# Second projection by token: 16 wide products, a copy and 8 transposes in place of 64 products

## What is computed

```python
p = h @ w_in                                  # 1024 -> 2176 columns
u_pool, c_val, c_gate, s_h, s_b, s_c = split(p)
y_a = pool_mixer(u_pool);  z = c_val * sigmoid(c_gate)
y_b = silu(layer_norm(depthwise31(z) + b_dw)) # 31 taps
y_c = s_b * depthwise3(s_c * s_h)             # 3 taps
x = x + concat[y_a, y_b, y_c] @ w_out
h = rms_norm(x);  ids, gates = top 16 of 8 heads' product keys of (h @ w_q)
x = x + sum_k gates_k * gelu(h . expert_u[ids_k]) * expert_v[ids_k]
```

## Time and profile before

| | |
|---|---|
| Median of 3 runs | 3525.51 us (3525.33 to 3532.18) |
| The profiled execution | 3508.12 us, span 3505.7 us |
| Mean granted PE clock | 0.825 of 2.4 GHz |
| PE busy | 2387.2 us (68%), 7990 matmul instructions |
| DVE busy | 2172.2 us (62%) |
| POOL busy | 2141.8 us (61%), 2176 gathers |
| ACT busy | 259.9 us (7%) |
| DMA | 1201.44 MB, mean 343 GB/s; the gather queue holds 86% of the 16 engines' span |

### The profile page before, as it was taken

How to read it: one execution, slowest core, us unless ns; L and a number is a source line. 1 busy time by engine, 2 the same in 40 slices (tenths; PEclk the granted TensorE clock), 3 DMA queues, 4 the chain that set the end, 5 groups by cost and what they waited for, 6 DMA issues and landing times.

```text
span 3505.7 us, 25147 instructions
## 1 busy us (share of the span) xinstructions
PE 2387.2 (68%) x7990; PEld 890.5 (25%) x7990; DVE 2172.2 (62%) x5644; ACT 259.9 (7%) x506; POOL 2141.8 (61%) x2184
## 2 busy tenths in 40 slices
PE   7123876577875875587978366748798764865498
PEld 6112323121311241123314121412332322111022
DVE  3988278866666775735467777772716787655500
ACT  3000100100000000000100100001010000000000
POOL 0365566656665655666566656565656675666665
PEclk9666898788987967798989688669899886878799
DMA  6587898999899989997897999799789899999998
GB/s 236 222 326 297 297 366 313 366 349 378 320 379 360 350 318 409 410 410 290 309 366 292 372 341 387 291 379 355 288 316 362 339 349 348 369 387 385 370 380 330
DMA packets 331598, 1201.44 MB, mean 343 GB/s; under 512 B 40898, under 2 KB 41290, under 8 KB 329418
## 3 DMA queue, kind: packets, MB, share of 16 engines
q0 software_dynamic: 313344, 1140.99, 86.0%
q1 hardware_dynamic: 17034, 49.94, 3.7%
q10 hardware_dynamic: 1088, 8.91, 0.6%
HBM read 1188.82 MB, written 10.87 MB: 342 GB/s over the span
## 4 chain that ended last, share of the span: by engine, by line
PE 23%; another core or an unknown queue 21%; POOL 18%; DVE 17%; issue 14%; DMA 5%; ACT 2%; ACTq 0%; DVEq 0%; POOLq 0%
POOL rows L590 18%; PE acc L974 11%; DVE rows L1420 8%; PE psA L807 4%; DMA rows<-in_expert_v,idsT 4%; PE psB L917 3%; PE psA L798 2%; DVE work L1149 1%; DMA rows<-in_expert_u,ids 1%; DVE work L1235 1%; DVE work L1228 1%; PE psB L834 1%; DMA w_in_sb<-in_w_in 1%; DVE work L1225 1%
## 5 line engine op out<-in xcount | busy, mean ns | idle before, releaser
L974 PE MATMUL acc<-rows,strip 128*32 128x512 f32 x4352 | 1558.1, 654 | 546.8 <-DMA rows<-in_expert_v,idsT 403.3
L1420 DVE CUSTOM_DVE_ANT_0 rows<-rows,psH 128x1024 f32<-128x1024 f32 x1088 | 1290.9, 1218 | 399.7 <-DMA rows<-in_expert_u,ids 296.3
L590 POOL DMA_INDIRECT rows<-in_expert_v,idsT x1088 | 1100.5, 1011 | 667.3 <-issue 268.3
L590 POOL DMA_INDIRECT rows<-in_expert_u,ids x1088 | 1040.3, 956 | 681.6 <-issue 317.3
L974 PEld LDWEIGHTS acc<-rows,strip 128*32 128x32 f32 x4352 | 349.1, 115 | 1633.3 <-issue 1038.4
L807 PE MATMUL psA<-hT,w_in_sb 128*128 128x128 f32 (+1 forms) x1280 | 203.1, 315 | 97.9 <-issue 97.1
L807 PEld LDWEIGHTS psA<-hT,w_in_sb 128*128 128x128 f32 x1280 | 190.6, 231 | 124.0 <-issue 124.0
L1149 DVE SCALAR_TENSOR_TENSOR work<-zbuf,chan,work 128x128 f32<-128x128 f32 (+1 forms) x870 | 215.2, 325 | 6.7 <-DVE work L1149 3.9
L798 PE MATMUL psA<-w_out_sb,hT 128*128 128x512 f32 x320 | 163.0, 651 | 32.7 <-ACTq L661 25.9
L1427 DVE TENSOR_TENSOR x_out<-acc,x_out 128x1024 f32<-128x1024 f32 (+1 forms) x10 | 12.2, 1221 | 266.0 <-PE acc L974 178.6
L917 PE MATMUL psB<-w_q_sb,hT 128*128 128x512 f32 x288 | 141.2, 640 | 31.7 <-remote 15.7
(11 more groups left out here) (181 smaller groups left out, 1287.5 us busy)
## 6 DMA issues: line engine op xcount, KB each, us to landing
rows<-in_expert_u,ids POOLq DMA_INDIRECT x1088
rows<-in_expert_v,idsT POOLq DMA_INDIRECT x1088
w_in_sb<-in_w_in ACTq DMA_DIRECT2D x4, 2176.0 KB, 17.6
w_in_sb<-in_w_in SPq DMA_DIRECT2D x4, 2176.0 KB, 18.6
w_out_sb<-in_w_out SPq DMA_DIRECT2D x2, 4096.0 KB
w_q_sb<-in_w_q SPq DMA_DIRECT2D x2, 4096.0 KB
x_out<-x_mid SPq DMA_DIRECT2D x10, 512.0 KB
x_mid<-x_mix SPq DMA_DIRECT2D x8, 512.0 KB
```

Of the source, the lines that this page charges most:

```text
L590: nc.gpsimd.indirect_dma_start(out=rows[:, j, :], out_offset=None, in_=table[:, :], in_offset=bass.IndirectOffsetOnAxis(ap=index, axis=0))\
L974: last = nc.tensor.matmul(acc[LS * a:LS * (a + 1), half:half + 512], strip[:, first:first + LS], rows[:, at % RING, half:half + 512], star ...
L1420: nc.vector.tensor_tensor_reduce(rows[:, j, :], rows[:, j, :], psH[:, :], 1.0, 0.0, ALU.mult, ALU.add, dots[:, r:r + 1]).then_inc(s_free[j ...
```

## The change

For tiles 1 to 9 the second projection is made by token, as the first one is: for each chunk k, two products of 128x512 with `hT` chunk k as weights (16 products in all), into `psA`. The yields stay. ACT then copies the 128x1024 result into `hT` (tick 9, `KEEP_B`, after `s_pC`, when PE reads `hT` no more), PE turns it back with 8 transposes into `psA` (tick 10, `TURN_B`, before `POOL_MIX`, with a `yield` between them), and the copy of `s_h` moves to tick 11 and waits for the transposes. Tile 0 stays as it was.

```diff
-CONV, PROJ_C, POOLING, SH_COPY, POOL_MIX, POOL_KEEP, SHORT, ... = 8, 8, 9, 9, 10, 11, 12, ...
+CONV, PROJ_C, KEEP_B, POOLING, TURN_B, POOL_MIX, SH_COPY, POOL_KEEP, SHORT, ... = 8, 8, 9, 9, 10, 10, 11, 11, 12, ...
```

```diff
-                if tick == SH_COPY:
+                if tick == KEEP_B and m:
                     act.wait_ge(s_pC, m + 1)
+                    nc.scalar.copy(hT[:, :, :], tri(psA[:, :])).then_inc(s_pBc, 1)
+                if tick == (SH_COPY if m else KEEP_B):
+                    if m:
+                        act.wait_ge(s_pB, m)
+                    else:
+                        act.wait_ge(s_pC, 1)
                     nc.scalar.copy(shc[:, :, 0:L], p_sh[:, :, 0:L]).then_inc(s_sh, 1)
```

```diff
-                if tick in (PROJ_B, PROJ_B + 1):
+                if m == 0 and tick in (PROJ_B, PROJ_B + 1):
                     for k in range(4 * (tick - PROJ_B), 4 * (tick - PROJ_B) + 4):
                         last = project(m, psA, D, k)
+                if m and tick in (PROJ_B, PROJ_B + 1):
+                    for k in range(4 * (tick - PROJ_B), 4 * (tick - PROJ_B) + 4):
+                        for half in (0, 512):
+                            nc.tensor.matmul(psA[:, half:half + 512], hT[:, k, :], w_in[:, k, D + half:D + half + 512],
+                                             start=k == 0, stop=k == DC8 - 1, skip_group_check=True)
                         if k < DC8 - 1:
                             yield
-                    if tick == PROJ_B + 1:
-                        last.then_inc(s_pB, 1)
...
+                if tick == TURN_B and m:
+                    pe.wait_ge(s_pBc, m)
+                    for c in range(DC8):
+                        last = turn(psA[:, c * P:(c + 1) * P], hT[:, c, :])
+                    last.then_inc(s_pB, 1)
+                    yield
                 if tick == POOL_MIX:
```

More of the change, by code:

```diff
@@ L23 @@
 NORM, NORM_ROWS, TURN_X, HT_SET, PROJ_A, PROJ_B, GATE_SIGMOID, HISTORY, GLU = 0, 1, 2, 3, 4, 6, 6, 6, 7
-CONV, PROJ_C, POOLING, SH_COPY, POOL_MIX, POOL_KEEP, SHORT, MEAN, CENTRE = 8, 8, 9, 9, 10, 11, 12, 12, 13
+CONV, PROJ_C, KEEP_B, POOLING, TURN_B, POOL_MIX, SH_COPY, POOL_KEEP, SHORT, MEAN, CENTRE = 8, 8, 9, 9, 10, 10, 11, 11, 12, 12, 13
 OUT_A, OUT_B, SQUARE, VAR, SCALE, SILU, REPEAT, OUT_C, STATES, X1 = 13, 14, 14, 15, 16, 17, 18, 18, 19, 19
@@ L346, in build @@
         s_pA = sem("first_projection_made")
-        s_pB = sem("second_projection_made")
+        s_pBc = sem("second_projection_by_token_copied")
+        s_pB = sem("second_projection_turned")
         s_pC = sem("third_projection_made")
```

## The result

The changed kernel takes 3487.12 us in the median of six runs (3480.56 to 3496.37). The kernel before took 3531.15 us in the six runs beside it (3525.33 to 3548.66). The ratio is 0.9879, with a 95% interval from 0.9857 to 0.9901: faster by about 43 us, between 35 and 50. The forecast was 3487.5.

A forecast was written before the change was run, and what follows sets the result against it. Gathers run at the DMA limit except where POOL waits, 244.8 us of it for slots PE held. Gains of 50 us less 12 added give 38, so 3525.5 - 38 = 3487.5 us, range 3452 to 3528.

The forecast's parts named there:

- The stall goes with the narrow form: Second projection, L807: 97.1 us of PE idle without shown cause goes with wide products, as only the narrow form stalled.
- B: Rival: the stall isn't of the narrow form, prompt tiles keep it, only sample tiles gain; 4 us, 3521; chance 0.12.
- Tiles 4 and 7 run 21 us shorter on PE and give 12 us each: Sample tiles' second projection: PE stretch from 39.0 to 18 us, POOL's two waits nearly go, DVE limits; 24 us together.
- Tiles 6 and 9 give 15 us: Prompt tiles 6 and 9: POOL's waits of 10.42 and 9.40 us go but for a remainder; gains 8 and 7.
- Tile 1 gives 8 us: Tile 1: POOL's 14.74 us wait goes, but DVE's taps then hold a gather, so only 8 us is gained.
- The added part costs 12 us: Copy and 8 transposes: 2.0 us of PE in each of six prompt tiles, 12 us; bounds 0 and 28.
- The sum: All tiles: 24 + 15 + 8 + 2 + 1 = 50 us gained, less 12 added, net 38 us.
- half of B: Share of rival B counted as 0.03 within the 0.76 chance of a time faster by more than 0.2%.
- SHORT in tiles 5 and 8 comes 10 us later, covered by MEAN: DVE's SHORT waits 10 us more, costed at nothing since its next step awaits MEAN; 2 x 10 us if uncovered.
- Rival C: Stalls stay and DVE reaches SHORT before TURN_B is through, `u` rows behind it: slower, 3556 us; chance 0.11.
- POOL's waits on PE fall from 245 to about 190: Sign to look for: POOL's waits for L974, slots that PE held, fall from 245 to about 190 us.
- No change of the time can come from the arithmetic of the prompt tiles: Prompt tiles, full clock: 128 narrow instructions 14.4 us, 32 wide 14.2, so they gain only if the stall goes.

The follow-up runs named there:

- second trace of the changed kernel: The changed kernel run again without an edit, against the kernel before: 3479.83 us against 3522.63, ratio 0.9874.
- second trace of before: The kernel before run again without an edit, against itself: 3519.95 us against 3529.66, ratio 0.9981.
- sample tiles alone: Only tiles 4 and 7 get the new path, the other tiles as in the kernel before: 3501.93 us, ratio 0.9918.
- added part alone: Kernel before with narrow products kept, plus copy, 8 transposes and later copy of `s_h`: 3524.54 us, ratio 1.0003; on the faster chips 3204.86 us, ratio 0.9995.

## Why the prediction was right, and where it was right by luck

The time, 3487.5, and the sign held on chips of the sort on which before was profiled. The mechanism held in part: PE's stretches became shorter as forecast and POOL's waits behind them went, but in the two tiles that gave most, 13 of PE's 20 us were pace, not idle time, and POOL's waits on PE elsewhere remain. Step by step:

**The stall goes with the narrow form.** Right. L858 has 0.0 us of idle time, four 128x128 in place of each 128x512 bring the stall back (122.5 us), and 128x256 brings 21.6 us. B's doubt was half justified all the same: something of the chip is needed too, since the same narrow form does not stall on the second sort. The prediction took the stall as a property of the form, and it is one of form and chip together. It also read the waits too narrowly. "Only the narrow one stalled" leaves out PE's `v` rows, 512 columns wide, with 116.1 us in 85 waits, and L917, which "had none", has 4.4 us in 2. The form makes the stall where the projection stands; it doesn't follow that a wide instruction can't wait in this way.

**Tiles 4 and 7 run 21 us shorter on PE and give 12 us each.** Right, and a little low. The stretch of tile 4 is 18.5 us where 18 was forecast. The granted clock over it went from 0.54 to 0.97. The stall alone had not kept it low: on the second sort PE was busy for 25.20 of the 25.30 us of the narrow products of tile 4, without a stall, and the clock over them was 0.71, in tile 7 even 0.58. POOL's waits on PE there, 10.83 and 11.85 us, are reduced to a single one of 2.31 up to 1340 us, in the timeline of POOL of the changed kernel:

```profile
1325.80 0.93 POOL L591 DMA_INDIRECT rows<-in_expert_u,ids  x1 [2.31 <-PE acc L990]
```

The start of the first projection in tiles 4, 5, 6, 7, 8 and 9 gives the length of one tile. First PE's timeline of before, then that of after:

```profile
1235.39 2.09 PE L834 MATMUL psB<-w_in_sb,hT 128*128 128x512 f32 x4
...
1556.80 1.98 PE L834 MATMUL psB<-w_in_sb,hT 128*128 128x512 f32 x4
...
1826.28 1.98 PE L834 MATMUL psB<-w_in_sb,hT 128*128 128x512 f32 x4
...
2160.12 2.23 PE L834 MATMUL psB<-w_in_sb,hT 128*128 128x512 f32 x4
...
2459.64 1.98 PE L834 MATMUL psB<-w_in_sb,hT 128*128 128x512 f32 x4 [1.79 <-issue]
...
2733.08 2.47 PE L834 MATMUL psB<-w_in_sb,hT 128*128 128x512 f32 x4
```

```profile
1237.69 1.98 PE L841 MATMUL psB<-w_in_sb,hT 128*128 128x512 f32 x4 [0.99 <-DVE hT L1147]
...
1546.52 2.25 PE L841 MATMUL psB<-w_in_sb,hT 128*128 128x512 f32 x4
...
1819.98 2.06 PE L841 MATMUL psB<-w_in_sb,hT 128*128 128x512 f32 x4
...
2149.20 2.98 PE L841 MATMUL psB<-w_in_sb,hT 128*128 128x512 f32 x4
...
2437.56 3.42 PE L841 MATMUL psB<-w_in_sb,hT 128*128 128x512 f32 x4 [3.32 <-DVE hT L1147]
...
2711.34 1.98 PE L841 MATMUL psB<-w_in_sb,hT 128*128 128x512 f32 x4
```

Tile 4 went from 321.4 to 308.8 us, tile 7 from 299.5 to 288.4: 13 and 11. The second trace of the changed kernel has 307.5 and 287.3 for the two, the second trace of before 322.8 and 298.9. The sample tiles alone measured 29 us for both, against 24.

**Tiles 6 and 9 give 15 us.** Too high as far as the traces tell. Tile 6 went from 333.8 to 329.2 us (start of tile 6 to start of tile 7), and from tile 9's start to the end of the span it was 772.6 us before and is 774.7 now. Their stretches did shorten as said (25.2 and 26.8 us), and no wait of POOL on PE is left within either. Tiles with the same code move by up to 10 us from trace to trace, however (tile 2 took 340.7 and 344.9 us in the two traces of before and 334.5 in the kernel with new sample tiles), so that the single values of tiles 2, 3, 5, 6, 8 and 9 can't be told apart by this.

**Tile 1 gives 8 us.** Nothing in one trace, 4 to 8 us in another. In the first the stretch is 65 us shorter, and the gather that follows the taps comes at 359.08, against the end of the taps' long gather at 343.11 + 13.56 = 356.67; by 360 us both kernels had issued 145 gathers. Timeline of the changed kernel, all engines, tile 1:

```profile
332.26 0.27 ACT L698 COPY coefT<-psH 128x128 f32<-128x128 f32 x1 [3.27 <-remote]
332.43 1.02 ACT L641 COPY hT<-psA 128x1024 f32<-128x1024 f32 x1
333.50 1.97 PE L766 MATMUL psA<-ident,hT 128*128 128x128 f32 x8 [3.62 <-ACT hT L641]
335.40 3.58 PE L990 MATMUL acc<-rows,strip 128*32 128x512 f32 x16
...
339.23 0.94 POOL L591 DMA_INDIRECT rows<-in_expert_v,idsT  x1 [8.95 <-PE acc L990]
339.76 18.20 DVE L1165 SCALAR_TENSOR_TENSOR work<-zbuf,chan,work 128x128 f32<-128x128 f32 x69 [0.16 <-DVE work L1188]
341.76 17.01 POOL L591 DMA_INDIRECT rows<-in_expert_v,idsT  x1 [0.30 <-issue]
```

POOL's wait fell from 14.74 to 8.95 us, but the `v` rows that free the first slots now stand behind copy and transposes: from 332.53, when the coefficients were copied, to 335.40, some 3 us of the wait. I had costed both at nothing in this tile, because "PE now has time to spare". It has, but not there: it waits for the coefficients until 332.5, and copy and transposes come after. What was won was then lost on the taps, which held one gather for 17.01 us. The prediction named that hold and still took 8.

The second trace of the changed kernel doesn't repeat the loss. POOL's timeline there:

```profile
335.43 2.68 POOL L591 DMA_INDIRECT rows<-in_expert_v,idsT  x1 [5.46 <-PE acc L990]
...
344.41 14.49 POOL L591 DMA_INDIRECT rows<-in_expert_v,idsT  x1 [2.56 <-PE acc L990]
```

Four gathers pass before the one that the taps hold, and 147 are out by 360 us, where the second trace of before has 143. The 200th gather is issued at 447.7 us, against 451.9 and 455.4 in the two traces of before and 452.8 in the first of the changed kernel. How much tile 1 gives thus depends on how many gathers pass before DVE's row of taps begins, and its mean wasn't measured.

**The added part costs 12 us.** Wrong by size: 1 us measured, -6 to +8, in a kernel that keeps the stall. The step that failed is that POOL waits for every 2 us that PE is later in the six prompt tiles. The lower bound, all of it under gathers in flight, was the nearer one.

**The sum.** Gross 50 less 12 gave 38; measured were 43 and nearly nothing for the added part, so the removed stalls and the faster pace together gave about 43. The terms of the prompt tiles, 26 us in all, are too high against the some 15 that are left beside the sample tiles, the term of tiles 4 and 7 was a little low and the cost too high. What was left of these errors, 5 us of gain, was cancelled by the base: the forecast stood on 3525.5, and the kernel before took 3531.15 in the runs beside the changed one. The hit within 0.4 us is luck. In the chances, "half of B" is 0.06 and was added as 0.03, a slip that changes nothing here.

**SHORT in tiles 5 and 8 comes 10 us later, covered by MEAN.** Right in size, not in every trace. In tile 5 it is not late at all in the first trace, where SHORT stands at 1615.43 with 0.22 us in front; in the second it has 11.11 us in front, and in the kernel with the added part alone 10.55, released by the copy of `s_h`. In tile 8 it is late by 9.57, and the step behind it waits for MEAN anyway, as said. Timeline of DVE of the changed kernel:

```profile
2518.42 0.42 DVE L1211 TENSOR_TENSOR mbuf<-psA,hT 128x256 f32<-128x256 f32 x1 [9.57 <-ACT hT L647]
...
2537.25 0.56 DVE L1384 SCALAR_TENSOR_TENSOR work<-psB,work 128x384 f32<-128x384 f32 x1 [14.80 <-remote]
```

The first row waits for the moved copy of `s_h`, the second is L1384, which needs MEAN, with 14.80 us of idle time that the view puts down to "remote". Rival C asked for `u` rows behind SHORT while it waits. There are none here, and the kernel with narrow products and the added wait together, C's own case, measured 1.0003.

**POOL's waits on PE fall from 245 to about 190.** 178.2, and 172.4 in the second trace of the changed kernel.

**No change of the time can come from the arithmetic of the prompt tiles.** Right: on the second sort of chip, where there is no stall, wide against narrow measured 0.0 to 0.1% over all tiles. On supply of instructions the Trainium skill (Runtime: NRT & Kernel Launch, Instruction fetch mechanics) says that it is mostly hidden. The second sort agrees, with 0.0 us of idle time at 1280 narrow instructions. The first sort showed 97.1 us of idle time that went with the number of instructions, so if the supply is what fails there, it is not hidden. No run here shows that it is the supply.

## What to carry to other kernels

Time that stands in front of a line as "issue" in a few tiles only, while another line of the same arithmetic has none, is worth a trial with fewer, wider instructions; a version in which only the width differs then tells form from place. A wait that a change removes is worth what the next engine leaves of it: balance all waits of the bounding engine before and after, in more than one pair of traces, as here 67 and 74 us less on PE bought 20 and 39. Split a shorter stretch into idle time and pace before naming its cause. And such a gain need not hold everywhere: where the stall was missing, each part of this change was worth nothing that could be measured, so look for the stall in a trace from each chip before calling the change good or useless.

## What the runs showed of the hardware that was not expected

**Two levels of time for one kernel.** One unchanged kernel, 3523 to 3531 us in one case and 3201 to 3204 in the other, 9% less. The kernel with the added part alone was traced in both: span 3514.7 against 3206.3 us, the same 1201 MB at 342 against 375 GB/s in the mean. The granted clock is 0.829 against 0.860, but PE is busy for only 37 us less (2369.8 against 2332.7) and POOL's busy time is the same within 6 us, so the clock doesn't explain 308 us. What differs are waits without a shown cause, on several engines. POOL has 333.8 us of "remote" in 234 waits in the one trace and none in the other, DVE 205 us of "issue" against 0, PE 448 against 5. None of the six traces taken on the second sort has a "remote" wait of POOL. What the waits are for, the profile does not say.

**The stall ends by itself when the gathers stop.** In tile 4 of before, three instructions in order of time, from the timeline of all engines:

```profile
1287.67 0.93 POOL L590 DMA_INDIRECT rows<-in_expert_u,ids  x1 [0.30 <-issue]
...
1291.08 0.21 PE L807 MATMUL psA<-hT,w_in_sb 128*128 128x32 f32 x1 [1.20 <-issue]
...
1291.78 3.82 PE L807 MATMUL psA<-hT,w_in_sb 128*128 128x32 f32 x17 [0.49 <-issue]
```

POOL issues its last gather at 1287.67 and then waits for a slot that PE holds. PE, which had taken single instructions with gaps of one to two us before them, runs 17 in a row from 1291.78 on, 3.2 us after that gather's instruction ended at 1288.60. Tiles 6, 7 and 9 of before show the same, with 3.1 to 3.5 us. So the stall seems to make its own end: PE starves while gathers are in flight, holds slots, POOL runs out of them, the gathers drain, PE recovers, and by then POOL has lost some 11 us. That would explain why the waits of POOL behind it are alike in these tiles. It is a reading of the traces of the first sort alone, and no run tests it. What PE lacks meanwhile stays open: not the weights of one buffer (the stall stays when the operands change places), not a share of full DMA engines as such (408 GB/s on the second sort without a stall, and tile 0 on the first). That the instructions themselves come late is an obvious rival, and no run settles it: the page's queue for instructions moved 63 packets before and 57 after, and 64 in the kernel with the added part alone on either sort, stall or none, which tells how much came and not when. Fewer bytes in flight on the first sort would have been the next experiment and weren't tried there.
